# Streaming-encoder trunk on eight cores: mixed tile order at the end of Fox, ScalarE evacuation of the first pair, per-tile waits and early output steps in HGRN2

## Time and profile before

| | |
|---|---|
| median of 3 runs | 3595.34 us (3595.16 to 3924.01) |
| the profiled execution | 3592.3 us, span of its slowest core 3591.3 us (cores 3582.7 to 3591.3) |
| TensorE busy | 3344.1 us, 93% of the span |
| VectorE, ScalarE, GpSimd busy | 1447.6, 1290.8, 156.2 us |
| mean granted TensorE clock | 0.978 |
| stages of the slowest core | Fox 0 to 455 us, SwiGLU to 920, HGRN2 to 1346, SwiGLU to 1811, Fox to 2227, SwiGLU to 2692, HGRN2 to 3114, SwiGLU to the end |

### The profile page before, as it was taken

How to read it: one execution, slowest core, us unless ns; L and a number is a source line. 1 busy time by engine, 2 the same in 40 slices (tenths; PEclk the granted TensorE clock), 3 DMA queues, 4 the chain that set the end, 5 groups by cost and what they waited for, 6 DMA issues and landing times.

```text
span 3591.3 us, 47292 instructions; the slowest of 8 cores (3582.7 to 3591.3 us)
## 1 busy us (share of the span) xinstructions
PE 3344.1 (93%) x17264; PEld 1604.9 (45%) x17264; DVE 1447.6 (40%) x2159; ACT 1290.8 (36%) x2067; POOL 156.2 (4%) x256
## 2 busy tenths in 40 slices
PE   6999999999888889999989898999998888899998
PEld 2444344444454434444445443444444554344443
DVE  6443521113467672111374445111145667611215
ACT  3666511002477741101236564110135776411013
POOL 1000000000000000000020000000000000000000
PEclk9999999999999999999999999999999999999999
DMA  5111132121122113112100110312201221131212
GB/s 130 22 19 24 18 62 40 31 47 27 19 33 36 19 30 59 34 31 47 24 15 13 31 30 13 64 28 43 42 15 30 36 33 30 18 64 33 38 30 94
DMA packets 42289, 131.00 MB, mean 36 GB/s; under 512 B 4448, under 2 KB 4704, under 8 KB 42048
## 3 DMA queue, kind: packets, MB, share of 16 engines
q0 software_dynamic: 33120, 110.54, 17.9%
q1 hardware_dynamic: 8944, 17.44, 1.5%
HBM read 229.90 MB, written 8.59 MB: 66 GB/s over the span
## 4 chain that ended last, share of the span: by engine, by line
PE 86%; ACT 5%; DVE 4%; issue 3%; DMA 1%; ACTq 0%; DVEq 0%; SPq 0%; POOLq 0%; POOL 0%
PE ps L304 32%; PE ps L421 11%; PE ps L507 11%; PE ps L314 10%; PE ps L884 9%; PE ps L817 4%; PE ps L754 3%; PE ps L342 2%; PE ps L646 2%; PE ps L933 2%; DVE hT_sb L360 1%; DVE xT_sb L426 1%; ACT U L799 1%; DVE U L1067 1%; ACT U L954 1%
## 5 line engine op out<-in xcount | busy, mean ns | idle before, releaser
L304 PE MATMUL ps<-hT_sb,ring 128*128 128x512 bf16 x5248 | 1134.0, 379 | 6.7 <-ACT U L484 6.7
L304 PEld LDWEIGHTS ps<-hT_sb,ring 128*128 128x128 bf16 x5248 | 513.2, 98 | 626.8 <-issue 8.5
L484 ACT ACTIVATE U<-ps 128x2048 bf16<-128x2048 f32 x88 | 165.2, 1877 | 1371.4 <-PE ps L304 1371.3
L487 DVE TENSOR_TENSOR U<-U,ps 128x2048 bf16<-128x2048 bf16 x84 | 192.1, 2287 | 950.2 <-PE ps L304 923.0
L884 PE MATMUL ps<-hT_sb,ring 128*128 128x512 bf16 x1536 | 377.1, 399 | 74.4 <-ACT U L945 45.8
L314 PE MATMUL ps<-hT_sb,ring 128*128 128x512 bf16 (+1 forms) x1728 | 410.0, 385 | 25.2 <-DVE U L624 11.1
L507 PE MATMUL ps<-U,ring 128*128 128x512 bf16 x1792 | 387.4, 379 | 0.0
L799 ACT ACTIVATE U<-ps 128x512 bf16<-128x512 f32 (+3 forms) x640 | 303.3, 536 | 208.5 <-PE ps L758 122.1
L421 PE MATMUL ps<-U 128*128 128x512 bf16 x1536 | 372.5, 383 | 3.8 <-DMA U<-c_out 2.6
L426 DVE TENSOR_TENSOR xT_sb<-xT_sb,ps 128x512 f32<-128x512 f32 x320 | 218.4, 686 | 206.3 <-PE ps L421 187.2
L332 ACT ACTIVATE U<-xT_sb 128x512 bf16<-128x512 f32 x288 | 177.7, 628 | 287.1 <-DVE xT_sb L426 274.7
(11 more groups left out here) (113 smaller groups left out, 2522.9 us busy)
## 6 DMA issues: line engine op xcount, KB each, us to landing
ring<-ffn_in POOLq DMA_DIRECT2D x88, 512.0 KB, 5.3
ring<-ffn_out POOLq DMA_DIRECT2D x16, 896.0 KB, 7.1
xT_sb<-xT SPq DMA_DIRECT2D x8, 1024.0 KB, 19.5
U<-ffn_out POOLq DMA_DIRECT2D x16, 512.0 KB, 12.1
yT<-xT_sb SPq DMA_DIRECT2D x16, 512.0 KB, 2.9
ring<-c_v POOLq DMA_DIRECT2D x14, 512.0 KB, 5.3
ring<-ab_qk POOLq DMA_DIRECT2D x8, 512.0 KB, 6.4
ring<-ab_cx POOLq DMA_DIRECT2D x8, 512.0 KB, 6.5
```

Of the source, the lines that this page charges most:

```text
L304: inst = nc.tensor.matmul(ps[0:m, banks[tt], :], lhsT=w.ap[:, kc, c0:c0 + m], rhs=hT[:, kc, tt * 512:(tt + 1) * 512], start=(kc == 0), sto ...
L487: T.op(DVE, lambda: nc.vector.tensor_tensor(out=v4(ubuf(jj, 1).ap), in0=v4(st.ap), in1=ps[:, 4:8, :], op=ALU.mult), reads=flat_res(st, ban ...
```

## The change

1. `Norm` takes its square and scale buffers by counters instead of by tile number, and keeps the scale buffer of each tile. `OutProj.step` remembers the order of final steps, so that tiles may finish interleaved, and applies two pieces per step when more than eight are due. `run` emits the applies that are due at once, ahead of the tail.
2. Fox: queries and keys of the first pair are evacuated by ScalarE.
3. Fox's output: the 16 last-chunk steps of t = 0 and 1 are interleaved with the eight full steps of t = 2, two to one; sums of squares go to banks 7, 3 and 4 by tile.
4. HGRN2: a projection item names only the pieces of its own token tile as read.
5. HGRN2: a slot without an item evacuates what is pending. Slots 120 to 123 do four output steps (t = 0, chunks 0 to 5) and the output weights are fetched ahead of head 7's query weights. The quarters of head 7 start every 3 slots instead of every 4. Slots 128 to 139 hold one step, 140 to 143 two, 144 to 147 none.

```diff
@@ Norm.square, Norm.ss, Norm.apply
-                sqb = self.sq[(t * 8 + c) % 4]
+                sqb = self.sq[self.nsq % 4]
+                self.nsq += 1
...
-                    rs = self.rs[t % 2]
+                    rs = self.rs[self.nrs % 2]
+                    self.nrs += 1
+                    self.rs_of[t] = rs
@@ OutProj.step
                 if last:
                     self.nm.square(t, dc)
-                    self.nm.apply(1)
-                    if self.i >= 2:
-                        self.nm.ss(*divmod(self.i - 2, NKC))
-                    self.i += 1
+                    self.nm.apply(1 if len(self.nm.todo) <= NKC else 2)
+                    self.done.append((t, dc))
+                    if len(self.done) > 2:
+                        self.nm.ss(*self.done.pop(0))
@@ OutProj.run
                 while self.order:
                     self.step(banks)
+                self.nm.apply()
@@ fox_layer, qk_items
-                        if which == 0:
+                        if g == 0:
+                            T.op(ACT, lambda: nc.scalar.activation(out=o, in_=i_, func=AF.Copy, scale=1.0 if which else 0.125),
+                                 reads=[bank[b]], writes=dst.res)
+                        elif which == 0:
@@ fox_layer, output
-                                 lambda jj, t: aout(jj, t) if jj < 4 else bout(jj - 4, t), gnext, [7], 32 * KB // 4096,
+                                 lambda jj, t: aout(jj, t) if jj < 4 else bout(jj - 4, t), gnext, [7, 3, 4], 32 * KB // 4096,
                                  [(t, dc, 0, 7) for t in range(2) for dc in range(8)]
-                                 + [(t, dc, 7, 8) for t in range(2) for dc in range(8)]
-                                 + [(t, dc, 0, 8) for t in range(2, 4) for dc in range(8)], [4, 5, 6, 7, 0, 1, 2, 3])
+                                 + [e for t in range(2) for k in range(4)
+                                    for e in ((t, 2 * k, 7, 8), (t, 2 * k + 1, 7, 8), (2, 4 * t + k, 0, 8))]
+                                 + [(3, dc, 0, 8) for dc in range(8)], [4, 5, 6, 7, 0, 1, 2, 3])
@@ hgrn_layer, proj_items and v_items
-                        T.op(PE, fn, reads=flat_res(w, h_res), writes=[bank[b]])
+                        T.op(PE, fn, reads=flat_res(w, ht_res[q]), writes=[bank[b]])
...
-                        T.op(PE, fn, reads=flat_res(w, h_res), writes=[bank[b]])
+                        T.op(PE, fn, reads=flat_res(w, ht_res[t2 // 2]), writes=[bank[b]])
@@ hgrn_layer, the slot table
-                    c0 = P0 + 4 * q
+                    last = n == 7
+                    c0 = P0 + (3 if last else 4) * q
...
+                    if last:
+                        lag, ln = -1, c0 + 23
                     put(c0 + 24 + lag, b_ss, n, q)
                     put(ln, b_norm, n, q)
                     put(ln + 1, b_ot, n, q)
-                    put(c0 + 22, b_pvi, n, q)
-                    put(c0 + 23, b_og, n, q)
+                    put(c0 + (21 if last else 22), b_pvi, n, q)
+                    put(c0 + (22 if last else 23), b_og, n, q)
@@ hgrn_layer, slots and output
             def slot(P, fl):
                 if fl:
                     pump(fl)
+                else:
+                    flush()
...
+            wring, wu = [], []
+            op = OutProj(lambda p: wring[p] if p < 2 else wu[p - 2], 8, lambda j, t: VO(j, t), gnext, [2], 12,
+                         [(0, dc, 0, 6) for dc in range(4)] + [(1, dc, 0, 7) for dc in range(4)]
+                         + [(t, dc, 0, 7) for t in range(2) for dc in range(4, 8)]
+                         + [(0, dc, 6, 8) for dc in range(4)] + [(0, dc, 7, 8) for dc in range(4, 8)]
+                         + [(1, dc, 7, 8) for dc in range(8)]
+                         + [(t, dc, 0, 8) for t in range(2, 4) for dc in range(8)])
...
+                    if n == 7 and src is None:
+                        wring += [W.get(("c_out", gl, p), c_out_d[ci, p], 8, 256) for p in range(2)]
                     for i in range(4):
+                        if n == 7 and src is None:
+                            flush()
+                            op.step([0, 1])
                         slot(16 * n + 4 * k + i, fl)
             flush()
...
-            for P in range(128, 150):
-                if P < 148:
+            for P in range(128, 148):
+                if P < 140:
                     op.step([0, 1])
-                if P in (144, 145, 146, 147):
+                elif P < 144:
+                    op.step([0, 1])
                     op.step([0, 1])
                 slot(P, [])
```

More of the change, by code:

```diff
@@ L326, in __init__ @@
                 self.todo = []
+                self.nsq = self.nss = self.nrs = 0
+                self.rs_of = {}
             def square(self, t, c):
@@ L339, in ss @@
                     return
-                sqb = self.sq[(t * 8 + c) % 4]
+                sqb = self.sq[self.nss % 4]
+                self.nss += 1
                 b = self.ssbanks[t % len(self.ssbanks)]
@@ L356, in apply @@
                     sl = slice(t * 512, (t + 1) * 512)
-                    rs = self.rs[t % 2]
+                    rs = self.rs_of[t]
                     fin = self.gcol == C_GFIN
@@ L403, in __init__ @@
                 self.nm = Norm(gcol, ssbanks, u0)
-                self.i = 0
+                self.done = []
                 self.nb = 0
@@ L441, in tail @@
                     self.nm.apply()
-                    self.nm.ss(3, 6)
-                    self.nm.ss(3, 7)
+                    for e in self.done:
+                        self.nm.ss(*e)
                     self.nm.apply()
@@ L1186, in hgrn_layer @@
                         fl = []
+                    if n == 7 and src is None:
+                        wring += [W.get(("c_out", gl, p), c_out_d[ci, p], 8, 256) for p in range(2)]
                     for i in range(4):
+                        if n == 7 and src is None:
+                            flush()
+                            op.step([0, 1])
                         slot(16 * n + 4 * k + i, fl)
             flush()
-            wring = [W.get(("c_out", gl, p), c_out_d[ci, p], 8, 256) for p in range(2)]
-            wu = []
-            op = OutProj(lambda p: wring[p] if p < 2 else wu[p - 2], 8, lambda j, t: VO(j, t), gnext, [2], 12,
-                         [(t, dc, 0, 7) for t in range(2) for dc in range(8)]
-                         + [(t, dc, 7, 8) for t in range(2) for dc in range(8)]
-                         + [(t, dc, 0, 8) for t in range(2, 4) for dc in range(8)])
-            for P in range(128, 150):
-                if P < 148:
+            for P in range(128, 148):
+                if P < 140:
                     op.step([0, 1])
-                if P in (144, 145, 146, 147):
+                elif P < 144:
+                    op.step([0, 1])
                     op.step([0, 1])
```

## The result

The fastest execution of the changed kernel, the profiled one, took 3556.25 us; that of the kernel before took 3592.3. Over the first comparison the ratio of the times is 0.9894, with an interval of 0.9865 to 0.9923, which is 38 us less (some runs of both kernels were disturbed on one half of the chip and are left out of every comparison here). The forecast was 3539.7 for the profiled execution and 3543 for the median.

What follows compares the result with a forecast made beforehand. TensorE, busy 93% of the span, was taken as the bound, so only its waits and slow stretches could be won: 22 + 11 + 7 + 12.6 = 52.6 off 3592.3 gives 3539.7, median 3543 us; range 3524 to 3559.

Steps and rivals of the forecast that it cites:

- the sum's frame: Whole kernel: everything between the edited stretches keeps its order and shifts unchanged, so the stretch gains add to 52.6 us.
- Start of HGRN2: First projection items of both HGRN2 layers: waits on other token tiles go; 22 us won, range 18 to 23.
- Start of Fox: Both Fox layers: sixteen copies a layer move from DVE to ScalarE; gains 7.6 and 3.6, sum 11, range 6 to 14.
- The chains: Gate chains on DVE at the second Fox layer's start: 6.2 us apart.
- Fox output: Interleaved output steps of both Fox layers: 31 to 33 us against 35.9 and 34.2; 7 us won, range -4 to 15.
- a triple: Fox output: one long step of t = 2 plus four single matmuls, 3.82 us instead of 2.8, through the square's latency.
- The half-clock rival: Mixed places: single matmuls between waits run at half clock, a triple takes 5.55 us; 3621 us, chance 0.03.
- End of HGRN2: Last slots of both HGRN2 layers: early flush, early steps and closer quarters win 12.6 us, range 0 to 27.
- I take 27.5 for the 12 slots: HGRN2 slots 128 to 139: 27.5 us, 4.5 less than 32 and 8.5 less than 36.
- TensorE alone bounds them: Mixed places: Fox output 27.5 us, HGRN2 slots 128 to 143 at 24.4; with the starts 75 won, 3520; chance 0.13.
- delay the first query item, which needs the bank of the fourth: HGRN2 slots 120 to 127: early steps hold back the query item and add 4 x 0.6 us to DVE.
- No wait for U<-c_out: HGRN2 end: sign that TensorE's wait for output weights, 2.64 us in the longer layer before, is gone.

## Why the prediction was wrong

**The failing step is the sum's frame:** "Everything between them keeps its order and is taken to shift unchanged." Order was kept, pace was not. A stretch of 160 us at 0.81 gives 20 to 27 us back on the pair that has it, and the time is the slowest core's. The kernel before has one in 27 of 172 pairs, the change in 21 of 44, eleven executions in all of which one was free of it (3536.1 us). On the cores without a stretch the change gives more than the sum: their mean goes from 3588 to 3530, 58 us for 52.6, and on core 0 of the two profiles the stages below add up to 64.5. On the slowest core 38 are left. No rival named this: the clock was priced only inside the stretches that the change touches, and the profile before showed no window at 0.81 in any core. That the measured 3556.25 lies inside the range of 3524 to 3559 is luck: the upper part of the range was there for stretches that win less than their sums, and on the undisturbed cores they win more.

The stages below are those of core 0, before and after.

**Start of HGRN2 (22 predicted): right.** From the stage's start to its last item 336.0 us before and 324.4 on core 0, 335.0 and 323.8 in the second layer: 11.6 and 11.2. The kernel with edits 1 and 4 alone gives undisturbed cores of 3556 to 3569 against 3580 to 3597 before, in the mean 26 less.

**Start of Fox (11): right, a little small.** The second layer reaches attention in 44.3 us for 52.5: 8.2 for 7.6. The chains stand where the steps said. The first gives 5.3 for 3.6. Taking edit 2 out of the kernel without early steps raises its undisturbed cores from 3525 to 3532 up to 3536 to 3545, 13 in the mean.

**Fox output (7): right in mechanism, and nearly in size.** From the end of attention to the last step 48.2 us for 52.5, 47.9 for 52.2: 8.6 in all, with 3.88 a triple for 3.82. The forecast's own terms do not give its 31 to 33 us, though: 4.2 + 1.0 + 7 x 3.82 + 1.7 + 0.4 is 34. In the trace only six such distances lie between the second and the eighth long step (2138.46 to 2161.93 us in the second layer), and t = 3 starts 30.9 us after the last attention matmul. The half-clock rival is refuted: the clock is 1.00 where 0.86 and 0.95 stood. The Trainium skill's rule on short idles that cycle through banks ("TensorE: Matmul & The Clock Gate", section "A second HAM failure mode: psum-queue depth-cycling") speaks of such places; idles of 0.91 us in each triple did not lower the clock here.

**End of HGRN2 (12.6): mis-sized, and the step that held the cost.** From the last item to the last output step 79.1 us for 89.4, 78.3 for 87.6: 19.6. The term that was mis-sized is "I take 27.5 for the 12 slots": from DVE's add of slot 128 to the first of slot 140 it took 24.0 and 23.9 us:

```profile
1236.13 0.67 DVE L432 TENSOR_TENSOR xT_sb<-xT_sb,ps 128x512 f32<-128x512 f32 x1
...
1260.10 1.28 DVE L432 TENSOR_TENSOR xT_sb<-xT_sb,ps 128x512 f32<-128x512 f32 x2
```

That is at the floors of 24.4 and 24.0, as the rival "TensorE alone bounds them" had it for this place. Slots 128 to 143 took 33.9 and 32.0 us on this core before, so the term gave 18 us where 13 were forecast. On this core some 4 us come without edit 5 (86.2 and 86.5 in the kernel without it), so edit 5 is worth 15; the first layer's end differs by some 6 us from core to core before, so this split is rough. The means of the undisturbed cores, 3544 without edit 5 and 3530 with it, say 13. I had written that the early steps "delay the first query item, which needs the bank of the fourth": this is the wait of 6.22 us, 4.89 without them. The steps were priced by DVE's 0.6 us an add, and not by the clock of what follows. And they earn nothing that shows: on core 0 the first layer's last output step starts at 1310.9 with them and 1311.2 without, the second's at 3044.2 and 3048.3, but over all undisturbed cores the mean is 3530 with them (3524.5 to 3535) and 3528 without (3524.6 to 3532). No wait for U<-c_out is left, as the steps said.

**The better version.** The change without its four early steps, 3530.7 and 3532.6 us at best and 3545 in the mean of six, beats both: 61 below the mean of before, where the change is 45 below it. The 16 us between them rest on six and eleven executions.

## What to carry to other kernels

Where the metric is the slowest core, read the span and the clock of every core, of several executions, before and after, and price a change on the cores that are alike; what a sum wins on one core can be given back on another. Ask of every filler not only whether it fits into the gap but what it makes wait on its bank: four steps that earned nothing measurable lengthened a pause of TensorE from 4.89 to 6.22 us, and with them in place half of all pairs of cores had a stretch that cost some 20 us or more, against 22 of 120 in the changed kernels without them there. And try the change without each of its parts, down to four lines: the part that earned least was the one that cost. Where windows suggest a cause, read the same place in order of time, and in a core that does not show the effect, before building the next kernel on it.

## What the runs showed of the hardware

- A third rate of TensorE: granted clock 0.81, 512-column matmuls 0.26 us apart in place of 0.216, mostly for some 160 us, in pairs of cores at a time, each costing its pair 20 to 27 us. One of 29 to 378 us cost its pair some 40.
- It begins at 29 to 35 or at 72 to 77 us in the first Fox layer, in the last slots of an HGRN2 layer (1233 to 1256 and, in one profile, 2989 us), and in one profile at 3360 us. At 72 to 77 us and in HGRN2 windows with TensorE idle or at 0.63 to 0.77 stand right ahead of it; at 3360 us TensorE was busy for 29.84 of 30 us at 1.00 ahead of it. The same pause with the same low clock stands in cores that stay at 1.00.
- Pairs of cores with identical programs and other data behave differently in one execution, and the same pair differently from one execution to the next.
